# Where a filler matmul group ends between the steps of two attentions on one Trainium2 core

## What is computed

```
h  = rms_norm(x)
c_q, c_kv, k_r, fq, fk, fv, f_logit, u, gate_logits = split(h @ w_in)
o_mla = causal attention, 4 heads, q/k of 96 (latent, with rope), v of 64
o_fox = causal attention, 4 heads, q/k of 64 and a cumulative log-forget bias
o_s5  = diagonal state-space branch over u
gates  = sigmoid(gate_logits)                     # 3 x 1024 columns
x = x + (sum over branches of gates * (branch @ w_branch)) @ w_out
x = x + conv-gated feed-forward of rms_norm(x)
```

## Time and profile before

| what | value |
|---|---|
| runs, median (lowest to highest) | 1565.25 us (1564.69 to 1566.06) |
| the profiled execution, its own time | 1569.25 us |
| its span, first to last instruction | 1567.2 us |
| mean granted TensorE clock | 0.983 of full |
| busy PE, DVE, ACT, POOL | 94%, 64%, 42%, 8% of the span |

### The profile page before, as it was taken

The page is one execution under the profiler, slowest core; times in us unless marked ns, Lnnn a source line. Parts: engine busy times, 40 slices in busy tenths (PEclk is TensorE's granted clock), DMA queues, the critical chain, the costliest instruction groups (busy, mean ns, idle before and its releaser), DMA issues. The chain is left out here.

```text
span 1567.2 us, 18982 instructions
## 1 busy us (share of the span) xinstructions
PE 1469.9 (94%) x7122; PEld 1229.9 (78%) x7122; DVE 998.9 (64%) x1378; ACT 657.7 (42%) x1058; POOL 125.5 (8%) x104
## 2 busy tenths in 40 slices
PE   5899999898998998998999978999999999999999
PEld 4899977776877776786778766888888888888887
DVE  4312165564685565884782457888888788669786
ACT  4231135453524453213552235555555555544332
POOL 2000040010230012210210000000000000000000
PEclk9899999999999999999999989999999999999999
DMA  5110231113121111323665112332222221693222
GB/s 203 45 59 1 107 96 37 34 30 132 33 88 34 32 40 49 108 56 115 213 202 189 41 41 68 97 92 81 82 81 81 85 90 55 242 362 148 74 82 74
DMA packets 128757, 147.88 MB, mean 94 GB/s; under 512 B 10970, under 2 KB 93837, under 8 KB 128397
## 3 DMA queue, kind: packets, MB, share of 16 engines
q1 hardware_dynamic: 128480, 146.63, 28.3%
q10 hardware_dynamic: 189, 0.08, 0.0%
HBM read 109.78 MB, written 36.31 MB: 93 GB/s over the span
## 5 line engine op out<-in xcount | busy, mean ns | idle before, releaser
L1842 PE MATMUL ps<-split_arena 128*128 128x512 f32 x1320 | 307.9, 390 | 4.4 <-DVE split_arena L2617 3.5
L516 PE MATMUL ps<-split_arena 128*128 128x512 f32 x1152 | 292.6, 403 | 16.7 <-ACT plain_arena L551 11.0
L1842 PEld LDWEIGHTS ps<-split_arena 128*128 128x128 f32 x1320 | 247.8, 188 | 56.9 <-DVE split_arena L2617 4.0
L516 PEld LDWEIGHTS ps<-split_arena 128*128 128x128 f32 x1152 | 212.6, 191 | 64.0 <-issue 19.9
L1842 PE MATMUL ps<-up_b,split_arena 128*128 128x512 f32 x528 | 129.4, 395 | 5.1 <-DVE split_arena L1770 4.9
L2025 ACT ACTIVATE down_ops<-down_all 128x1024 fp32r<-128x1024 f32 x77 | 81.6, 1061 | 115.5 <-PE ps L2151 113.7
L2044 DVE TENSOR_TENSOR down_ops<-down_all,down_ops 128x1024 fp32r<-128x1024 f32 x77 | 94.1, 1224 | 46.3 <-ACT down_ops L2025 46.1
L1842 PEld LDWEIGHTS ps<-up_b,split_arena 128*128 128x128 f32 x528 | 100.6, 191 | 26.7 <-DVE split_arena L1770 5.2
L2149 PE MATMUL ps<-down_ops 128*128 128x512 f32 x308 | 119.9, 389 | 0.5 <-DVE down_ops L2044 0.5
L2151 PE MATMUL ps<-down_ops 128*128 128x512 f32 x308 | 119.8, 389 | 0.0
L2150 PE MATMUL ps<-down_ops 128*128 128x512 f32 x308 | 119.8, 389 | 0.0
(11 more groups left out here) (357 smaller groups left out, 2537.5 us busy)
## 6 DMA issues: line engine op xcount, KB each, us to landing
plain_arena<-in_w_in SPq DMA_DIRECT2D x24, 512.0 KB, 4.0
scr_gate<-plain_arena SPq DMA_DIRECT2D x48, 256.0 KB, 2.0
plain_arena<-scr_gate SPq DMA_DIRECT2D x24, 512.0 KB, 4.2
plain_arena<-in_w_up SPq DMA_DIRECT2D x22, 512.0 KB, 5.2
up_raw<-in_w_up SPq DMA_DIRECT2D x22, 512.0 KB, 5.0
scr_act<-plain_arena SPq DMA_DIRECT2D x22, 512.0 KB, 2.7
down_all<-scr_act SPq DMA_DIRECT2D x18, 512.0 KB, 9.4
down_all<-in_w_down SPq DMA_DIRECT2D x18, 512.0 KB, 10.4
```

The costliest lines, as they stand in the source:

```text
L516: mm = nc.tensor.matmul(m.ps[:, self.banks[half], :], w[:, k, :], src[:, k, h * BANK:(h + 1) * BANK], start=(j == 0), stop=(j == self.PER_ ...
L1842: mm = nc.tensor.matmul(o, self.w[j][w][:, k, :], self.h[j][k][h], start=(j in self.OPENS and k == 0 and n == 0), stop=(k == self.HK - 1 a ...
```

## The change

The gate matmuls of a head are spread differently over its steps: 6 in each of steps 0 to 5, then 4 ahead and 4 in step 6, 2 ahead and 2 in step 7. So the first half is complete with the last matmul of step 3, and its successor begins in step 4. In steps 4 to 7 ACT gets a `copy_made` behind its `fill.scalar`, ahead of the last high part of the step. Only in step 7 is there a complete half at that place: its copy moves there from the start of ACT's next step (for the last head, from the end of ACT's program). The first half's copy keeps its place in ACT's order, ahead of the exponent that opens step 4.

```
-ATT_FILL = (7, 7, 7, 6, 6, 5, 4, 2)
+ATT_FILL = (6, 6, 6, 6, 6, 6, 4, 2)
-ATT_AHEAD = (0, 0, 0, 0, 0, 0, 4, 0)
+ATT_AHEAD = (0, 0, 0, 0, 0, 0, 4, 2)
-assert sum(ATT_FILL) + sum(ATT_AHEAD) == UNIT
+assert sum(ATT_FILL) + sum(ATT_AHEAD) == UNIT and 2 * (sum(ATT_FILL[:4]) + sum(ATT_AHEAD[:4])) == UNIT
...
             if first:
                 self.fill.scalar(act, ATT_FILL[i])
+                self.fill.copy_made(act)
             self.split_hi(act, last)
             if not first:
                 self.fill.scalar(act, ATT_FILL[i])
```

## The result

The changed kernel took 1548.63 us in the median (1546.06 to 1551.35), against 1565.65 for the kernel before, measured beside it: a ratio of 0.9888 with a 95% interval of 0.9866 to 0.991. That is 17.0 us less, where 16.4 were forecast; the forecast of 1549 started from 1565.25, and the median came out 0.4 us under it. Measured again beside some of the experiments it came to 1548.6, a ratio of 0.9901 (0.9884 to 0.9919).

The account below looks back on a forecast made before the run. PE was taken as the busiest engine, idle a tenth of the forgetting attention in waits. Terms 4.8 + 8.5 + 4.3 - 1.2 = 16.4 us off the 1565.25 us median gave 1549, range 1546 to 1556.5.

Parts of the forecast that it names:

- Step 0: Earlier copy ends PE's wait before the gate matmuls: 0.80 us in three heads of each attention, 4.8 us.
- Step 3: Half ends with this step, so six matmuls run without a wait: 1.06 us in eight heads, 8.5 us.
- Rival 2: Step 3's copy wait moves into step 4 and the 8.5 us go: 1557.4 us, chance 0.05.
- Matmuls out of steps 0 to 2: Three leave per head at 0.24 us each; step 1's gains nothing in three heads: 18 x 0.24 = 4.3 us.
- Matmuls into steps 5 and 7: One enters step 5, two go ahead in step 7; PE's waits for DVE hide them: zero cost.
- The last head: No q or k to transpose, so two matmuls and the copy delay its end: 0.6 us per attention, -1.2.
- The sum: All terms for both attentions: 4.8 + 8.5 + 4.3 - 1.2 = 16.4 us.
- rival 5: Shift changes a slow-clock stretch at the latent attention's start: 1.7 us either way, 1547 to 1551; no separate chance.
- Rival 1: Handshakes between DVE, ACT and PE hold part of the gain: 1557 us, chance 0.23.
- rival 3: Waits named for ACT are of something else, gain goes into DVE's waits: 1565 us, chance 0.03.
- rival 4: Copy in step 7 blocks ACT and all behind it, making the kernel slower: 1568.4 us, chance 0.02.

Follow-up runs that it names:

- e1: Kernel before with its old lists, only step 7's copy moved ahead of the last high part: 1564.2 us, ratio 0.9996.
- e4: Changed kernel with 8 gate matmuls in step 1 and 5 each in steps 2 and 3: 1551.3 us.
- e3: Changed kernel with the two matmuls ahead of step 7 moved one each into steps 4 and 5: 1551.0 us.
- e11: Changed kernel with two matmuls moved from step 4 to ahead of step 7, which has four there: 1552.0 us.
- e2: Changed kernel with the new lists but step 7's half copied at the start of ACT's next step, as before: 1559.0 us, ratio 0.9962.
- e6: e1 with 26 mask matmuls more in the first attention's first scores, about 1.6 us of work: 1560.9 us, ratio 0.9971.
- e5: The changed kernel itself measured once more, nothing altered: median 1548.6 us, both attentions 264.2 us.

## Why the prediction was right

- **Step 0.** Put at 0.80 us in six heads. The matmuls follow 0.14 us after the single transposition, not 0.03, so it was 0.69. The 0.03 came from a transposition followed by a values product, which was the wrong neighbour; this term was 0.7 us too large in all. That the copy would fit into ACT's idle time was right (0.41 of the 0.90 us is left), and e1 shows the term alone: 4.6 us, of which 0.3 are from the ends of the attentions.
- **Step 3.** Put at 1.06 us, measured 1.05 (2.52 - 1.47), and the room in step 4 at 0.9, measured 0.86. Rival 2 didn't come. The exponent behind the copy came 1.7 us later against PE, where 1.2 were reckoned, and was covered all the same.
- **Matmuls out of steps 0 to 2.** In step 2 the wait took up the one of step 1, in three heads, and no more (the bracket grew by 0.25, from 0.33 to 0.58); e4 shows why. The first head gained 1.7 us (31.01 to 29.31), where 3 x 0.24 + 1.06 = 1.78 were expected; the two next 2.19 and 2.14, where 2.34 were, the difference being mostly step 0's.
- **Matmuls into steps 5 and 7.** Free in inner heads. For step 5: from its mask to step 6's transposition the third head takes 4.13 us before and after (330.03 to 334.16, 321.77 to 325.90), with a matmul more. For step 7: 0.74 and 0.73 us from mask to transposition, shown from the other side by e3 and e11.
- **The last head.** Put at -0.6. The two matmuls took 0.52 (L696 of step 6 to L649: 1.44 us before, 1.96 after) and the copy 0.05 (from that L649 to the last values product 2.94 us before, 2.99 after). But the end behind the last values product got 0.23 us shorter (5.42 to 5.19), which I had counted at nothing: there the copy and its store no longer come last. The runs show it: with the copy at its old place (e2) the end takes 5.43 us, with it earlier alone (e1) 5.18. This term's net was -0.3, not -0.6, per attention. Calling that end nothing was the weakest step of the prediction.
- **The sum** for the attentions was 16.4, measured 16.0. Step 0's term was 0.7 too large and the loss in the last heads 0.5 too large, and these two misses nearly cancel; the other terms were 0.2 too large together.
- **The median** came within 0.4 us of the forecast, and that is partly luck. The attentions give 16.0 of the 17.0 us. The rest hangs on the clock, and the changed kernel happened to keep that of the kernel before (0.987 and 0.9855 against 0.986). The medians of e2 and e4 show 5.5 and 5.3 us less gain than their attentions; with such a clock the 16.0 us would have shown as some 11 (my estimate from those two).
- **The clock** (rival 5) was right in kind and too small in size. I allowed 1.7 us either way for one stretch; the rest of the span differed by 10.6 us between the extremes of thirteen profiled executions. The Trainium skill (TensorE: Matmul & The Clock Gate, Part 1: The HAM clock gate) says that the number of slow matmuls changes from run to run with where the kernel stands against the chip's watch; that it changes is what two traces of the same kernel show, with mean clocks of 0.982 and 0.989; that the watch is the cause no run here shows.
- **Rival 1** (that handshakes take a part), rival 3 and rival 4 (ACT blocked by the copy) didn't come; the nearest thing to rival 4 is the last head's 0.05 us.

What stays open: why the executions of e1, e2, e4 and e11 get a lower mean clock than those of the kernel before, and not as often a higher one. e6 shows that 1.6 us of matmuls ahead of the first attention changes it; whether by their place in time or by the work they give PE isn't shown, and with one profile of most kernels I can't say which of the stretches are the usual ones.

## What to carry to other kernels

Where one engine is the busiest and all engines follow fixed orders, its idle brackets can be priced one by one: ask of each what the released work hangs on, and whether that moves too. A filler is worth the most if it is put where the busy engine waits for a chain that doesn't depend on what it does there (here steps 1, 6 and 7), and if its own handover (the copy of its bank) ends at a place where other work lies between. Measure such an edit by its stage in the trace as well as by the whole time: a gain of 4.6 us was there in the attentions and not in the run.

## What was unexpected

The stretches at 1.2 GHz outside the attentions are worth up to 10.6 us of 1285, with identical instructions: 0.010 in the mean clock is 31 us at half of it, of which a third shows as time (both worked out from the spans and clocks of e1 and e5). Whether a gain of a few us shows in the median can depend on 1.6 us of matmuls ahead of them (1564.2 against 1560.9).
